# A two-block transformer kernel: the opening in another order (inputs first, modulation by feature tile, w_k by feature tile, eight weight rows later)

## What is computed

```python
sh1x, sc1x, g1x, sh2x, sc2x, g2x = split(silu(c) @ w_ada + b_ada, 6)      # for x
sh1c, sc1c, ...                  = split(silu(c_ctx) @ w_ada + b_ada, 6)  # for ctx
hc = rms_norm(ctx, norm1_g) * (1 + sc1c) + sh1c
hx = rms_norm(x, norm1_g) * (1 + sc1x) + sh1x
k, v, lr of hc and of hx;  u, vs, q, r, ga, gb of hx       # all by h @ w_in
la = log_sigmoid(lr @ gla_w2 + gla_b2) / 16                # the "logits", two directions
# gated linear attention in chunks of 64 over q, k, v, exp(cumsum(la));
# spatial gating: u * (sgu_w @ layer_norm(vs) + sgu_b); merge, residual, convolution MLP,
# then the second block (gated delta rule, short convolution, two MLPs)
```

## Time and profile before

| | |
|---|---|
| median of 3 runs | 1244.25 us (1243.69 to 1245.8) |
| span of the profiled execution | 1243.2 us |
| PE busy | 1223.5 us, 98% |
| POOL busy | 880.3 us, 71% |
| DVE busy | 736.0 us, 59% |
| ACT busy | 722.2 us, 58% |
| moved by DMA | 217.76 MB, 175 GB/s in the mean |
| granted PE clock, mean | 0.993 |

### The profile page before, as it was taken

The page is one execution under the profiler, slowest core; times in us unless marked ns, Lnnn a source line. Parts: engine busy times, 40 slices in busy tenths (PEclk is TensorE's granted clock), DMA queues, the critical chain, the costliest instruction groups (busy, mean ns, idle before and its releaser), DMA issues.

```text
span 1243.2 us, 26081 instructions
## 1 busy us (share of the span) xinstructions
PE 1223.5 (98%) x9026; PEld 1127.9 (91%) x9026; DVE 736.0 (59%) x1718; ACT 722.2 (58%) x1325; POOL 880.3 (71%) x387
## 2 busy tenths in 40 slices
PE   9999999999999999999999999999999999999997
PEld 3678899988998888889999999999999999999986
DVE  3989972244587774159884375555634757555633
ACT  3656654565666665479642366666655547666753
POOL 0357857568869888957533248888898868888795
PEclk9999999999999999999998999999999999999999
DMA  9995355446646665645332126555566555656562
GB/s 369 408 366 186 102 187 153 119 149 205 183 142 210 190 186 164 188 146 162 118 98 75 52 88 190 182 183 172 159 187 196 174 166 170 193 180 185 154 200 71
DMA packets 66038, 217.76 MB, mean 175 GB/s; under 512 B 9904, under 2 KB 17328, under 8 KB 62624
## 3 DMA queue, kind: packets, MB, share of 16 engines
q1 hardware_dynamic: 65952, 216.59, 55.0%
HBM read 215.52 MB, written 1.05 MB: 174 GB/s over the span
## 4 chain that ended last, share of the span: by engine, by line
issue 38%; POOL 37%; PE 22%; ACT 1%; POOLq 1%; DVE 1%; ACTq 0%; DVEq 0%
POOL w_lo L673 36%; PE bank L802 10%; PE bank L1135 5%; PE bank L894 3%; PE bank L903 1%; PE bank L898 1%; POOL w_lo L680 1%; POOLq L670 0%; ACT h L1689 0%; ACT w_hi L1689 0%; POOLq L672 0%; PE bank L948 0%; PE bank L724 0%; PE bank L729 0%; PE bank L725 0%
## 5 line engine op out<-in xcount | busy, mean ns | idle before, releaser
L673 POOL TENSOR_TENSOR w_lo<-w_raw,w_hi 128x1024 fp32r<-128x1024 f32 x340 | 812.8, 2404 | 325.1 <-ACT w_hi L1689 323.7
L1689 ACT ACTIVATE w_hi<-w_raw 128x1024 fp32r<-128x1024 f32 (+1 forms) x372 | 378.1, 1020 | 103.0 <-PE bank L903 34.8
L802 PE MATMUL bank<-a_hi,w_hi 128*128 128x264 f32 (+3 forms) x704 | 200.5, 285 | 0.6 <-DVE a_lo L3670 0.6
L802 PE MATMUL bank<-a_hi,w_lo 128*128 128x264 f32 (+3 forms) x704 | 200.2, 284 | 0.0
L802 PE MATMUL bank<-a_lo,w_hi 128*128 128x264 f32 (+3 forms) x704 | 199.9, 284 | 0.0
L802 PEld LDWEIGHTS bank<-a_hi,w_hi 128*128 128x128 f32 x704 | 132.9, 189 | 0.8 <-DVE a_lo L3670 0.8
L802 PEld LDWEIGHTS bank<-a_lo,w_hi 128*128 128x128 f32 x704 | 132.9, 189 | 0.1
L802 PEld LDWEIGHTS bank<-a_hi,w_lo 128*128 128x128 f32 x704 | 132.9, 189 | 0.0
L3745 DVE SCALAR_TENSOR_TENSOR bank<-row_mean,cols,bank 128x260 f32<-128x260 f32 (+3 forms) x112 | 54.6, 488 | 115.8 <-ACT cols L1689 113.0
L763 PE MATMUL bank<-a_parts,w_hi 128*128 128x256 f32 x448 | 81.5, 284 | 0.5 <-DVE a_parts L2952 0.4
L894 PE MATMUL bank<-g_parts,w_hi 128*128 128x512 f32 x308 | 78.9, 396 | 0.0
(11 more groups left out here) (548 smaller groups left out, 2933.1 us busy)
## 6 DMA issues: line engine op xcount, KB each, us to landing
w_raw<-in_s SPq DMA_DIRECT2D x284, 512.0 KB, 3.6
w_raw<-in_down SPq DMA_DIRECT2D x48, 512.0 KB, 3.5
adaw<-in_w_ada SPq DMA_DIRECT2D x16, 1024.0 KB, 9.7
w_raw<-in_down SPq DMA_DIRECT2D x24, 384.0 KB, 3.3
adab<-in_w_ada_first SPq DMA_DIRECT2D x8, 1024.0 KB, 8.7
ctxt<-in_ctx SPq DMA_DIRECT2D x1, 1024.0 KB, 11.3
x<-in_x SPq DMA_DIRECT2D x1, 1024.0 KB, 15.3
out_h<-h SPq DMA_DIRECT2D x4, 256.0 KB, 2.6
```

Of the source, the lines that this page charges most:

```text
L673: pool.tensor_tensor(w_lo[:, s], w_raw[:, s], w_hi[:, s].bitcast(F32), ALU.subtract) \
L802: ins = mm(banks[bank][:, tk], w_[:, s, k], x_[:, k, tk], start=(m == 0), stop=(m == 3 * KD - 1))
L1689: return nc.scalar.activation(out_, in_, f, **kw)
```

## The change

The order of the opening is written anew, and some weights travel in another form.

- SP issues ctx and x (and only what they need) ahead of the modulation columns. The first 2 MiB of these come in four quarters, so that feature tile 0 has its columns first. w_k's weight comes in four pairs of feature tiles between them. w_k and w_q are rounded and multiplied in blocks, like w_v (`GROUPS` is 7).
- The modulation product is made for one feature tile at a time (`mod_rows(k)`), with the eight contraction tiles on four column groups: outputs in partitions 32g and 32g + 1. `flip_rows(k)` adds the four groups up. The mean squares are made in column groups too, the roots for 64 columns on 128 partitions, and `over_tokens` spreads them.
- PE runs `k_and_rank(k)`: the four w_k tiles and the low-rank product of feature tile k, with the flip of k + 1 and the modulation product of k + 2 among them. 24 opening and 12 filling products (`keep_warm`) stand where there were 16.
- w_q follows (`queries_by_blocks`): tiles 0 and 1 whole, then tiles 2 and 3 by feature tile, with the eight logits between the steps. The first w_v group has none any more.
- ACT rounds `w2s` and makes four silu tiles (two for the banks, two into `silu_c` for later) before w_q's blocks 6 and 7.
- Of the 16 rows eight (`ROWS_EARLY`) are used before the keys, five behind `normed_vs(1)` and before the spatial product, three behind the gating. PE waits for 13 rows before the spatial product, ACT for 15 before w_ga. On SP the later rows stand between the units of w_r.

The diff, cut to its core (removed lines are left out nearly everywhere):

```diff
+        ADA_RING = [IN_S, IN_VX, IN_VC, IN_S, IN_H, IN_S, IN_H, IN_S,
+                    IN_GA, IN_KD, IN_KS, IN_GA, IN_KD, IN_KS, IN_GA, IN_KD]
+        ROWS_IN_V, ROWS_EARLY, ROWS_IN_BANKS = 3, 8, 13
...
+            def group_block(g, j):
+                u, ks_ = SLOTS * g, slice(2 * j, 2 * j + 2)
+                if g:
+                    sp.wait_ge(block_lo, 8 * (g - 1) + 2 * j + 2)
+                sp.dma_start(w_raw[:, :, ks_], a["s0"][u:u + SLOTS, :, ks_].rearrange("o p k m -> p o k m")) \
+                    .then_inc(landed[j], 16)
+            n_pv = PV["norm1_g"] + KD
+            small(averages[:, 0], a["averages"][:, 0], ctx_in)
+            small(ctxt[:], a["ctx"], ctx_in)
+            small(pv[:, 0:n_pv], a["pv"][:, 0:n_pv], x_in)
+            small(x[:], a["x"], x_in)
             for j in range(4):
                 if j >= 2:
...
+                    sp.wait_ge(ada_done, 2 * j - 2)
                 for half in range(2):
...
+                    if j == 0:
+                        for part in range(2):
+                            own = slice((2 * part + half) * P, (2 * part + half + 1) * P)
+                            sp.dma_start(adab[0][:, :, own], a["w_ada_first"][0][:, :, own]).then_inc(ada_in[0][half], 16)
+                    else:
+                        ks_ = slice(4 * half, 4 * half + 4)
+                        sp.dma_start(adab[j % 2][:, ks_], a["w_ada_first"][j][:, ks_]).then_inc(ada_in[j % 2][half], 16)
+                    if half == 0:
+                        group_block(0, j)
...
+                    for j in range(3):
+                        group_block(1, j)
                     ada_rows(0)
...
+                    sp.wait_ge(split_ready, 8 * S_X + KD)
+                    ada_rows(1)
+                    ada_rows(2)
+                    for j in range(4):
+                        group_block(2, j)
+                    ada_rows(3)
+                    sp.wait_ge(z_done, 2 * HG)
+                    ada_rows(4)
+                    group_block(3, 0)
+                    ada_rows(5)
+                    for j in range(1, 4):
+                        group_block(3, j)
+                    for j in range(4):
+                        group_block(4, j)
+                    sp.wait_ge(csil_ready, 5)
+                    small(sguw[:], a["sgu_w"], stage_in)
+                    group_block(5, 0)
+                    ada_rows(6)
+                    group_block(5, 1)
                     ada_rows(7)
...
+                    for j in range(2, 4):
+                        group_block(5, j)
+                    sp.wait_ge(sc_done, 2)
                     ada_rows(8)
...
+                    sp.wait_ge(sc_done, 4)
+                    sp.wait_ge(kt_done, 8)
+                    ada_rows(9)
+                    ada_rows(10)
+                    slot_units(32, 35)
+                    ada_rows(11)
+                    slot_units(35, 36)
+                    ada_rows(12)
+                    slot_units(36, 38)
+                    ada_rows(13)
+                    ada_rows(14)
+                    slot_units(38, 40)
+                    ada_rows(15)
+                    first = 10
...
...
+            def mod_rows(k):
+                j, kk = divmod(k, 2)
+                if k:
+                    pe.wait_ge(gain_ready, k)
+                for c in range(KD):
+                    if j == 0 and c == 0:
+                        pe.wait_ge(ada_in[0][kk], 32)
+                    elif kk == 0 and c % 4 == 0:
+                        pe.wait_ge(ada_in[j % 2][c // 4], (0, 16, 48, 32)[j])
+                    g = 32 * (c % 4)
+                    cols = adab[j % 2][:, c].rearrange("p (part kk m) -> p part kk m", part=2, kk=2)[:, :, kk]
+                    ins = mm(banks[7][g:g + 2, 0:2 * P].rearrange("p (part m) -> p part m", part=2), c2[:, c], cols,
+                             start=(c < 4), stop=(c >= 4))
                 ins.then_inc(ada_done, 1)
...
+            def k_and_rank(k):
+                pe.wait_ge(split_ready, 8 * S_X + k + 1)
+                pe.wait_ge(block_lo, k + 1)
+                for s in range(4):
+                    if k == 0:
+                        pe.wait_ge(banks_free, s + 1)
                     for i, (w_, x_) in enumerate(((w_hi, a_hi), (w_hi, a_lo), (w_lo, a_hi))):
                         ins = mm(banks[s][:, :], w_[:, s, k], x_[:, k], start=(k == 0 and i == 0), stop=(k == KD - 1 and i == 2))
...
+                    if k == KD - 1:
+                        ins.then_inc(unit_used, 1)
+                    elif s == SLOTS - 1:
+                        ins.then_inc(block_used, 1)
+                    if s == 0 and 0 < k < KD - 1:
+                        flip_rows(k + 1)
+                if k == 0:
+                    pe.wait_ge(wlr_split, 1)
+                for i, (w_, x_) in enumerate(((wlr_hi, a_hi), (wlr_hi, a_lo), (wlr_lo, a_hi))):
+                    ins = mm(banks[6][0:96, :], w_[:, k], x_[:, k], start=(k == 0 and i == 0), stop=(k == KD - 1 and i == 2))
+                if k == KD - 1:
+                    ins.then_inc(lr_done, 1)
+                elif k < KD - 2:
+                    mod_rows(k + 2)
+            pe.wait_ge(ctx_in, 32)
+            mean_square(RMS_CTX)
+            keep_warm(8)
+            mean_square(RMS_X)
+            pe.wait_ge(warm, 3)
             mod_rows(0)
...
+            over_tokens(RMS_CTX)
+            over_tokens(RMS_X)
             flip_rows(0)
...
+            mod_rows(1)
...
+            def queries_by_blocks():
+                u0, t0 = UNIT0["w_q"], TILE0["w_q"]
+                def product(s, k):
+                    pe.wait_ge(block_lo, 2 * u0 + k + 1)
+                    b, c0 = Q_HOME[s]
+                    for i, (w_, x_) in enumerate(((w_hi, a_hi), (w_hi, a_lo), (w_lo, a_hi))):
+                        ins = mm(banks[b][:, c0:c0 + N1], w_[:, s, k], x_[:, k, 0:N1], start=(k == 0 and i == 0), stop=(k == KD - 1 and i == 2))
+                    return ins
+                pe.wait_ge(modrow_ready, KD)
+                pe.wait_ge(gain_ready, KD)
+                for s in range(2):
+                    for k in range(KD):
+                        ins = product(s, k)
+                    ins.then_inc(unit_used, 1)
+                for k in range(KD):
+                    for s in range(2, 4):
+                        if k == 0:
+                            pe.wait_ge(banks_free, t0 + s + 1)
+                        ins = product(s, k)
+                        if k == KD - 1:
+                            ins.then_inc(unit_used, 1)
+                        elif s == SLOTS - 1:
+                            ins.then_inc(block_used, 1)
+                    if k == 0:
+                        pe.wait_ge(lr_ready, 1)
+                        pe.wait_ge(rank_lo, 1)
+                    elif k == 1:
+                        pe.wait_ge(banks_free, t0 + 2 + 4)
+                    logits(k)
+            queries_by_blocks()
+            by_blocks("w_v", 4, 0)
             by_blocks("w_v", 4, 1)
...
+                    token_root(RMS_CTX)
+            token_root(RMS_X)
+            mod_rows(0)
+            blocks(0, 0, 1)
             mod_rows(1)
             modulated(0)
...
+            act.wait_ge(wlr_in, 16)
+            fn(wlr_hi[:], wlr[:], ACT.Copy).then_inc(rank_hi, 1)
+            blocks(0, 1, 2)
             modulated(1)
...
+            for k in range(2, KD):
+                mod_rows(k)
+                blocks(0, k, k + 1)
+                modulated(k)
+            blocks(1, 0, 6)
+            act.wait_ge(w2_in, 96)
+            fn(w2s[:], w2[:], ACT.Copy).then_inc(rank_hi, 1)
+            act.wait_ge(small_in, 64)
             act.wait_ge(split_ready, 8 * S_X + KD)
             for b in range(2):
                 fn(banks[4 + b][:, :], csil[:, b * 512:(b + 1) * 512], ACT.Silu).then_inc(csil_ready, 1)
...
+            for b in range(2):
+                fn(silu_c[b][:], csil[:, b * 512:(b + 1) * 512], ACT.Silu).then_inc(csil_ready, 1)
+            blocks(1, 6, 8)
+            act.wait_ge(lr_done, 1)
+            fn(lrs[:], banks[6][0:96, :], ACT.Copy).then_inc(rank_hi, 1)
+            for t in range(4):
+                act.wait_ge(unit_used, UNIT0["w_k"] + t + 1)
+                fn(k1[:, t], banks[t][:, :], ACT.Copy).then_inc(banks_free, 1)
...
+            def evac_q(t):
+                act.wait_ge(unit_used, UNIT0["w_q"] + max(t, 1) + 1)
+                fn(q1[:, t], banks[Q_HOME[t][0]][:, Q_HOME[t][1]:Q_HOME[t][1] + N1], ACT.Copy, scale=DK ** -0.5).then_inc(banks_free, 1)
             nc.scalar.preload_act_table_set("natural_log_exp_and_others")
+            evac_q(0)
+            evac_q(1)
             for i in range(2 * HG):
                 d, hh = divmod(i, HG)
                 act.wait_ge(z_done, i + 1)
                 fn(ebuf[:, d, hh], banks[6 + i % 2][:, :], ACT.Abs, bias=column("gla_b2", i)).then_inc(z_abs, 1)
+                if i >= 2:
+                    blocks(2, i - 2, i - 1)
+            evac_q(2)
```

(24 more changed lines are left out.)

399 lines of the change are left out of this document (151 added, 248 removed).

## The result

| | before | changed kernel |
|---|---|---|
| median of the runs | 1244.88 us (6, 1243.69 to 1245.94) | 1250.55 us (6, 1247.96 to 1251.93) |
| profiled span | 1243.2 us | 1250.1 us |
| ratio to before, 95% interval | | 1.0043 [1.0032, 1.0054] |

The change costs 5.7 us in the medians, where I had forecast a gain of 5.5. The profiled execution is the longest of the six: its span is 6.9 us above that of before.

What follows compares the result with a forecast made beforehand. From 39.90 us PE was taken as the bound, so its start and holes set the end. Span: 1243.2 - 6.8 + 1.3 = 1237.7; adding 1.05 gave 1238.8 us, chance 0.47, own range 1236.5 to 1241.

Steps and rivals of the forecast that it cites:

- the start of w_k: Opening: transfers, squares, roots and first modulation products added up to w_k starting at 19.4 us instead of 39.9.
- the losses behind the mark: After w_v starts: 0.5 us at w_u's first units and 0.8 at w_r's unit 35, 1.3 us in all.
- the mark: Start of the 192 w_v products, shared by both kernels: forecast 76.6 us against 83.4, 6.8 us gained.
- I keep the rate of the others: Opening transfers: the first modulation block, in runs of 128 numbers, was priced at 2.48 us for each MiB.
- the other bound that I gave: First modulation block's transfers: twice their time, 2.5 us on the start.
- a rival of 2 to 3.5 us at 0.15: Clock falls as w_k starts, after short products: 2 to 3.5 us at half speed, 1241.5; chance 0.15.
- The loop: w_k over feature tiles: 4.9 us a tile on PE, modulation products 1.04, flips 0.41, low-rank product ending at 56.5 us.
- the hole: At w_q's first tile: PE waits about 5 us for blocks 6 and 7, behind w2s and four silu tiles.
- the eight steps: In w_q: eight steps of two tiles and a logit, about 1.15 us each on ScalarE, 9.0 us.
- (c): w_r on SP: rows 11 to 15 between units 35 to 40 each wait for a VectorE buffer; 0.8 us charged.
- the "slower" rival: w_r stage: rows on SP hold up the units, landing in 9.7 us; 10 us lost, 1249; chance 0.08.
- Late rows in SBUF: Last three rows' SBUF multiplications hold up GpSimd: 3 to 4 us lost (8.2 by the skill's rule), 1242.5; chance 0.10.

Runs made afterwards that it cites:

- e1: Changed kernel with the first modulation block transferred in two ordinary halves, the first weight block behind both; ratio 1.0052 to the kernel before.
- e6: Changed kernel with first modulation block in two halves, first modulation product behind the spreading products, 20 fillers before w_k; ratio 1.0020 to the kernel before.
- e2: Changed kernel plus 12 filler products between the first flip and second modulation product, and 2 before the second flip; ratio 1.0022 to the kernel before.
- e9: Changed kernel plus 13 filler products of zeros ahead of products 4, 5 and 6 of the first w_q tile; ratio 1.0029 to the kernel before.
- e4: Changed kernel with w_r's weight units 35 to 39 ahead of modulation rows 11 to 15 on SP, as slots allow; ratio 1.0068 to the kernel before.
- e10: Changed kernel with nine of the twelve multiplications of the last three modulation rows left out, rows still transferred; ratio 1.0038 to the kernel before.
- e8: Changed kernel with e6's edits, w_q's blocks earlier, group 3's blocks ahead of row 5, three more order edits; ratio 0.9958 to before, median 1239.4 us.
- e12: e6 with the first modulation block back in the changed kernel's four transfers of 512-byte runs; ratio 1.0034 to the kernel before.

## Why the prediction was wrong

The predicted span was 1237.7 us, the measured one 1250.1: 12.4 us. The steps that failed are the start of w_k (19.4 us forecast, 25.57 measured), the clock, which the sum put at nothing in two places, and the losses behind the mark (1.3 us forecast, 5.5 measured). Step by step:

1. **The start, up to the second modulation product: 4.5 us.** Forecast 16.1 us, measured 20.59. Three terms were too small. x was there at 10.43 us and not at 9.6: 0.8. From there the first gain, for which the second product also waits, was made at 18.33, 7.9 us later and not 6.5: 1.4, nearly all of it in the token roots' spreading, which was through 4.1 us behind the last square (13.18 to 17.24) where I had 2.8; it stands behind the first modulation product on PE. Only the last 2.2 us, from 18.33 to 20.59, are the transfer's. There the step said "I keep the rate of the others". The queue had 303 GB/s instead of 408 while these transfers ran, and SP was held 13 us by six issues (3.57 to 16.90). Even as halves (e1) the block ended 6.6 us after x (10.4) where its 2 MiB at that rate are 5.1; that what is issued behind it takes bandwidth from it is my reading, which no run isolates. For the transfer by itself the other bound that I gave, 2.5 us, held. From product to w_k the step was right: 3.3 us forecast, 3.33 in e6 (20.16 to 23.49).
2. **The clock at the start: 2.9 us** (e2; 1.2 to 2.8 by the other traces). The sum put it at nothing. I had it as a rival of 2 to 3.5 us at 0.15. It should have been a term: a standstill of 3.0 us among products of 2 and 64 columns brought it down here, and in e1 one of 2.75. I counted fillers against it without asking whether they stand where PE waits; with step 1's wait, they don't.
3. **The loop: right in mechanism, 1.0 us too short.** The product over column groups takes 1.04 us, as taken from the earlier trace rows, and all six in the loop do. A tile takes 5.08 us, not 4.90: counted from start to start, the modulation product with the changes on both sides of it 1.18 and not 1.04, the flip with its restart 0.45 and not 0.41. The Trainium skill (TensorEngine Tiling (Array Packing), Key Properties) states that a change of tiling mode drains TensorE. I had estimated 3.5 us more for that; the six products here have 0.8 more than the sum gave them, so a drain of that size doesn't show.
4. **w_q: 1.5 us.** From the low-rank end to w_v I had 20.1 us, and it was 21.6. The hole was 3.7 us, not 5, and the eight steps took 8.4 us, not 9.0, so these two were if anything priced too high. What was not in the sum is the clock that falls in the hole: the second w_q tile, with no wait in it, took 4.7 us (73.67 to 78.37) and not 2.9. By e9 the clock costs 2.0 in all.
5. **Behind the mark: 5.5 us lost, not 1.3.** Between the mark and the scores it was 2.7 us. The two waits in w_v cost 2.2 of them (0.33 and 1.55 us and the restarts) and were not foreseen. I had looked at each place where a block or unit stands behind a row and named w_u and w_r, and passed over group 3, whose blocks stand behind row 5. Between the scores and the second state product 0.8 went, of which PE's wait of 0.37 is one part. The w_r stage took 2.0 us instead of 0.8 (1.1 to 2.3 in the other runs with its order); the mechanism (c) was the right one, and the "slower" rival built on it had the right place and five times the price.
6. **Late rows in SBUF: right that they cost little**, for half of the reason. I expected GpSimd to be held up; VectorE was. The Trainium skill (SBUF — State Buffer, on its two separate sides) says that one of such a pair blocks the other for a whole instruction. VectorE's six multiplications of 2.8 us agree in kind: each waited for a remainder. Strict turns would need 0.68 + 2.40 = 3.1 us for a pair, and a pair took 2.8, so not all of it was exclusive. GpSimd lost 2.3 us over the six (16.71 against 6 x 2.40), not the 8.2 of the rule's reading in the prediction. VectorE had the time: its chain ended at 239.9 us, 0.6 us behind ScalarE's last square, and PE waited for neither.
7. **Given back: 2.0 us.** In the stretch of small products behind 650 us the clock falls in both kernels, for longer before (0.93 and 0.97) than after (1.00 and 0.93). Before:

```profile
650.00:700.00 50.00, 49.44 (x484) 47.21 (x484) 21.44 (x43) 14.92 (x26) 14.31 (x7) 0.93 0.25 75
700.00:750.00 50.00, 48.70 (x406) 47.16 (x406) 30.18 (x71) 29.26 (x54) 21.91 (x10) 0.97 0.27 84
```

The changed kernel:

```profile
650.00:700.00 50.00, 49.13 (x554) 46.81 (x553) 26.21 (x47) 17.35 (x30) 17.75 (x8) 1.00 0.23 76
700.00:750.00 50.00, 48.70 (x401) 47.15 (x400) 27.59 (x66) 23.09 (x40) 15.57 (x8) 0.93 0.23 75
```

Nothing of the change reaches there but the shift in time. Why it falls for longer in one of them wasn't tested and stays open. e4 and e10, which have the changed kernel's work there, show 0.93 and 0.97, as before does, so the pattern isn't tied to the kernel, and the 2.0 us need not come from the change.

Sum: w_k's start 6.2 (4.5 and 1.7 of the clock's 2.9), its first tile 1.4 (about the rest of the clock), the loop 1.0, w_q 1.5, behind the mark 4.2, less 2.0: 12.3 of the 12.4 us. One check in the prediction doesn't close either: 20.5 us of earlier start less 8.7, 0.8 and 5 is 6.0, not the 6.8 that the marks gave.

The idea of the change was sound and its mark reachable: e8 has it at 76.83 us, where I had said 76.6. That the two agree is partly luck, since e8 gets there another way: w_k starts at 23.27 us and not at 19.4, and from the last low-rank product to w_v it takes 16.8 us. The mark wasn't reached because of two standstills of PE, each with the clock's fall on top, a start that was late for more reasons than the transfer, and the order on SP.

## What to carry to other kernels

Price a wait of PE of some 3 us at its own length plus what follows at the lower clock: here 3.0 us of waiting brought 2.9 more at the start, and 3.7 brought 2.0 at w_q, in other traces 1.2 and 1.0 at the least. And where one queue issues both bulk rows and weight blocks, list every block that stands behind a row which waits for a buffer, not only those of the stage in view. A mended cause can show no gain (e1) while the next one holds: try them together before one of them is dropped. And before a gain is put down to an edit, look whether the difference is there already ahead of it (e6 and e12).

## What the runs showed of the hardware

- With the first modulation block in runs of 512 bytes the queue moved 303 GB/s from 9 to 19 us, with runs of 8 KB 408 (e1), and SP's issues took 0.8 to 4.8 us each. The Trainium skill (DMA: Bandwidth & Descriptors, Specifications) gives 512 bytes as enough for line rate; by that the short runs would have kept the rate, and the measurement decides.
- Behind waits of PE of 2.75 and 3.0 us in the opening the clock stood at 0.50, and behind 2.35 us at the spatial product (e4) it was down too (0.66 in 211 to 216 us). Fillers that add nothing held it at 1.00 in both places tried (20 to 30 us in e2, 70 to 80 in e9).
- VectorE's multiplication of two SBUF operands took 0.68 us alone and 2.8 beside GpSimd's subtraction, whose own length rose from 2.40 to 2.79 us. In e10 tiny VectorE operations on 32 columns and fewer, 0.2 us otherwise, took 2.2 us beside the same remainders.
